# First mixers begin with two value units on unnormalised x, exact x made behind them; operands in PSUM, low parts cut to width

## What is computed

```python
def first_block(x, ...):                 # cut
    for l in range(2):
        x = x + 0.5 * swiglu(rmsnorm(x, ffn1_norm[l]), ffn1_w_in[l], ffn1_w_out[l])
        x = x + hybrid_mixer(rmsnorm(x, mix_norm[l]), w_in[l], ...)
        x = x + 0.5 * swiglu(rmsnorm(x, ffn2_norm[l]), ffn2_w_in[l], ffn2_w_out[l])

def second_block(x, mem, ...):           # cut
    for l in range(2):
        x = x + hybrid_mixer_2(rms_norm(x, mix_norm[l]), ...)
        x = x + memory_cross_attention(rms_norm(x, mem_x_norm[l]), mem, ...)
        x = x + conv_gated_ffn(rms_norm(x, ffn_norm[l]), ...)
    return rms_norm(x, final_norm)
```

## Time and profile before

| | |
|---|---|
| Median of 3 runs | 2544.12 us |
| Lowest, highest | 2541.17, 2551.29 us |
| The profiled execution | 2547.06 us |
| Its span on the core | 2545.1 us |
| Granted TensorE clock, mean | 0.98 |
| Busy over the span | PE 95%, PEld 89%, POOL 70%, ACT 44%, DVE 42% |

### The profile page before, as it was taken

How to read it: one execution, slowest core, us unless ns; L and a number is a source line. 1 busy time by engine, 2 the same in 40 slices (tenths; PEclk the granted TensorE clock), 3 DMA queues, 4 the chain that set the end, 5 groups by cost and what they waited for, 6 DMA issues and landing times.

```text
span 2545.1 us, 44193 instructions
## 1 busy us (share of the span) xinstructions
PE 2414.0 (95%) x17548; PEld 2261.2 (89%) x17548; DVE 1067.2 (42%) x1686; ACT 1117.8 (44%) x1255; POOL 1787.8 (70%) x1368
## 2 busy tenths in 40 slices
PE   7999999998999999999999899999899999899998
PEld 7998888997999899898889799998788999788997
DVE  4224555323422332345553242223425664423865
ACT  4334434446433433444443644345444335455333
POOL 6998444455799899864445678987446998545996
PEclk9999999999999999999999999999999999799999
DMA  6554322323455455442223345564224655323553
GB/s 232 178 184 151 111 94 92 105 94 116 149 188 191 161 191 188 153 141 95 90 93 108 125 133 166 181 202 121 89 95 133 198 181 159 100 71 112 180 191 115
DMA packets 312188, 359.88 MB, mean 141 GB/s; under 512 B 18636, under 2 KB 291072, under 8 KB 311936
## 3 DMA queue, kind: packets, MB, share of 16 engines
q1 hardware_dynamic: 311866, 358.01, 43.3%
q10 hardware_dynamic: 198, 0.06, 0.0%
HBM read 357.00 MB, written 1.05 MB: 141 GB/s over the span
## 4 chain that ended last, share of the span: by engine, by line
POOL 60%; issue 34%; PE 4%; ACT 1%; POOLq 1%; DVE 0%; DMA 0%; ACTq 0%; DVEq 0%
POOL sb_lo L483 60%; PE ps L516 4%; POOLq L490 0%; DMA sb_hcol<-in_dn_a_log 0%; POOLq L492 0%; ACT sb_hT_h L1139 0%; ACT L1125 0%; ACT L1124 0%; ACT sb_kT L1131 0%; ACT sb_hi L1366 0%; ACTq L354 0%; ACT sb_hi L1120 0%; DVE sb_qT L2134 0%; DVE sb_levels L2067 0%; DVE sb_levels L2072 0%
## 5 line engine op out<-in xcount | busy, mean ns | idle before, releaser
L483 POOL TENSOR_TENSOR sb_lo<-sb_raw,sb_hi 128x512 fp32r<-128x512 f32 x1364 | 1787.6, 1346 | 734.7 <-ACT sb_hi L1120 733.8
L516 PE MATMUL ps<-sb_hT_h,sb_hi 128*128 128x256 f32 x3268 | 946.3, 290 | 30.3 <-ACT sb_levels L1182 6.1
L1120 ACT ACTIVATE sb_hi<-sb_raw 128x2048 fp32r<-128x2048 f32 x341 | 652.2, 1914 | 728.4 <-PE ps L516 697.4
L516 PE MATMUL ps<-sb_hT_h,sb_lo 128*128 128x256 f32 x3268 | 927.5, 284 | 0.0
L516 PE MATMUL ps<-sb_hT_l,sb_hi 128*128 128x256 f32 x3268 | 927.4, 284 | 0.0
L516 PEld LDWEIGHTS ps<-sb_hT_h,sb_hi 128*128 128x128 f32 x3268 | 627.8, 192 | 46.6 <-issue 23.0
L516 PEld LDWEIGHTS ps<-sb_hT_h,sb_lo 128*128 128x128 f32 x3268 | 628.6, 192 | 3.6 <-issue 1.4
L516 PEld LDWEIGHTS ps<-sb_hT_l,sb_hi 128*128 128x128 f32 x3268 | 628.0, 192 | 0.0
L516 PE MATMUL ps<-sb_hi,sb_o_h 128*128 128x512 f32 (+1 forms) x848 | 305.6, 360 | 8.9 <-DVE sb_o_l L1671 3.0
L516 PE MATMUL ps<-sb_hi,sb_o_l 128*128 128x512 f32 (+1 forms) x848 | 302.1, 356 | 0.0
L516 PE MATMUL ps<-sb_lo,sb_o_h 128*128 128x512 f32 (+1 forms) x848 | 301.4, 355 | 0.0
(11 more groups left out here) (341 smaller groups left out, 3139.8 us busy)
## 6 DMA issues: line engine op xcount, KB each, us to landing
sb_raw<-in_ffn_w_in SPq DMA_DIRECT2D x88, 1024.0 KB, 5.1
sb_raw<-in_w_in SPq DMA_DIRECT2D x78, 1024.0 KB, 5.2
sb_raw<-in_ffn_w_out SPq DMA_DIRECT2D x44, 1024.0 KB, 4.9
sb_raw<-in_ffn_w_up SPq DMA_DIRECT2D x44, 1024.0 KB, 5.1
sb_raw<-in_ffn_w_down SPq DMA_DIRECT2D x22, 1024.0 KB, 4.9
sb_raw<-in_w_out SPq DMA_DIRECT2D x16, 1024.0 KB, 5.1
sb_raw<-in_w_branch_a SPq DMA_DIRECT2D x8, 1024.0 KB, 5.1
sb_raw<-in_w_branch_b SPq DMA_DIRECT2D x8, 1024.0 KB, 5.1
```

Of the source, the lines that this page charges most:

```text
L483: ins = nc.gpsimd.tensor_tensor(lo[:, slot, c], raw[:, slot, c], hi[:, slot, c].bitcast(F32), ALU.subtract)
L516: ins = mm(dst, s, m, start=first and n == 0, stop=last and n == 3 * len(pairs) - 1)
L1120: fn(hi[:, slot, :], raw[:, slot, :], ACT.Copy).then_inc(hi_ready, 1)
```

## The change

Line numbers of the new kernel are higher than the old ones.

**Entry.** The first FFN of a block also turns x inside its last down unit. ACT and DVE make high and low parts of gain times x in `o_h`, `o_l` (shifted by four blocks, `UNSCALED_AT`, since the last down unit reads the low ones). PE runs sv0 and sv1 on them, token by token; ACT applies the root when it takes them out, one scale per partition. Meanwhile x with gain and root is made in `exact` (an alias of `qT`) by DVE from the turned x still in PSUM and `row`, and ACT and DVE split it into `hT_h`, `hT_l` for the other units. `tok` scaled, the 16 later turns and the 20 warming transposes go away.

**Order.** `FIRST` is now sv0, sv1, q0, z0, b, k0, a, v0, q1: nine units, with q1 taken from the first round of `delta`. b's and a's chain stands between the convolutions of k0 and v0.

**PSUM.** `prod`, the silu of the second blocks, the roots of `pre_roots`, the merge, the output of `delta` and the decay row work in PSUM where they stood in SBUF.

**Widths.** `split` and the low parts run over the columns a unit has; POOL's loop over the ring is written out.

```diff
-FIRST = [("b", 0), ("a", 0), ("sv", 0)] + pair_units(0) + [("sv", 1)]
-DELTA_BG = [pair_units(1) + [("sv", 2), ("sv", 3)], pair_units(2) + [("sq", 0), ("sk", 0)],
+FIRST = [("sv", 0), ("sv", 1), ("q", 0), ("z", 0), ("b", 0), ("k", 0), ("a", 0), ("v", 0), ("q", 1)]
+DELTA_BG = [pair_units(1)[1:] + [("sv", 2), ("sv", 3)], pair_units(2) + [("sq", 0), ("sk", 0)],
...
+def mix1_width(r):
+    return KB * mix1_unit(r)[3] if r < MIX1_UNITS else UNIT
+MIX2_WIDTHS = [2048, 1280, 1536, 1536, 2048, 2048, 2048, 1152, 768] + [UNIT] * 12
...
-        sil, prod = xinv, yinv
+        sil, conv_sil, prod = xinv, ps[:, 2, :], ps[:, 3, :]
+        exact = qT
...
+            for u, width in enumerate(WIDTHS):
+                if u == 0:
+                    continue
+                slot = u % RING
+                pool.wait_ge(hi_ready, u + 1)
+                if u < RING:
+                    pool.wait_ge(lo_ready, RING + u)
+                pieces = -(-width // (UNIT // PIECES))
+                for i in range(pieces):
+                    c = slice(width * i // pieces, width * (i + 1) // pieces)
...
+            def unscaled_part(b, k, bank, q, k0, k1):
+                if k0 == 0:
+                    arrived(b, k)
+                w = weights(k, KB, 256)
+                for t in range(ST):
+                    tt_ = slice(t * P, (t + 1) * P)
+                    for c in range(k0, k1):
+                        if t == 0 and c % 2 == 0:
+                            pe.wait_ge(h_ready, 4 * q + (c // 2 + 1))
+                        for n, (o, wt) in enumerate(((o_h, w[0]), (o_l, w[0]), (o_h, w[1]))):
+                            ins = mm(ps[:, bank, t * S:(t + 1) * S], o[:, (c + UNSCALED_AT) % KB, tt_], wt[:, c, :],
...
             def mixer1(l, b, q):                                  # PE
+                unscaled_part(b, 0, 0, q, 0, 4)
+                pe.wait_ge(x_ready, updates(q))
+                for g in range(2, 4):
+                    turn(g, AFTER_FFN_BANKS[g])
+                unscaled_part(b, 1, 1, q, 0, 4)
+                turn_row(3 * l + 1, AFTER_FFN_ROW)
+                unscaled_part(b, 0, 0, q, 4, KB)
+                unscaled_part(b, 1, 1, q, 4, KB)
+                pe.wait_ge(bank_free[0], BANK_UNITS[0] * l + 1)
+                arrived(b, 2)
...
+                                pe.wait_ge(exact_low, 4 * l + (c // 2 + 1))
...
-                ffn(2 * l, b, sil_ready, 2 * NCH * l)
-                transposes(3 * l + 1, l)
+                ffn(2 * l, b, sil_ready, 2 * NCH * l, 3 * l + 1)
...
             def mixer1(l, b, gain):                               # ACT
+                take_row(q, AFTER_FFN_ROW)
+                for g in range(4):
+                    act.wait_ge(exact_ready, 4 * l + (g + 1))
+                    sl = slice(2 * g, 2 * g + 2)
+                    fn(hT_h[:, sl, :], exact[:, sl, :], ACT.Copy).then_inc(exact_high, 1)
+                    if g == 1:
+                        evac1(l, 0)
+                        mix_split(b, 3)
+                evac1(l, 1)
...
-                rsqrt(levels[:, 2:4, :], ps[:, 2:4, :], 1.0 if half < NPAIR else 1.0 / P).then_inc(pre_act, 1)
+                rsqrt(ps[:, 2:4, :], ps[:, 2:4, :], 1.0 if half < NPAIR else 1.0 / P).then_inc(pre_act, 1)
...
             def mixer1(l, b):                                     # DVE
+                exact_pair(0)
+                for g in range(4):
+                    if g < 3:
+                        exact_pair(g + 1)
+                    dve.wait_ge(exact_high, 4 * l + (g + 1))
+                    c = slice(2 * g, 2 * g + 2)
+                    tt(hT_l[:, c, :], exact[:, c, :], hT_h[:, c, :].bitcast(F32), ALU.subtract).then_inc(exact_low, 1)
...
                 elif kind == "wb":                                # DVE, evac1
-                    tt(k2(t1), vT[:, sl, :], src, ALU.mult).then_inc(bank_free[bank], 1)
-                    freed(l, r)
-                    own.link(tt(k2(t2), k2(t1), zT[:, sl, :], ALU.add))
-                    halve(o_h[:, sl, :], o_l[:, sl, :], k2(t2)).then_inc(merged_ready, 1)
+                    own.link(tt(src, vT[:, sl, :], src, ALU.mult))
+                    own.link(tt(src, src, zT[:, sl, :], ALU.add))
+                    halve(o_h[:, sl, :], o_l[:, sl, :], src).then_inc(merged_ready, 1)
+                    dve.wait_ge(merged_ready, NPAIR * l + (int(c) + 1))
+                    dve.sem_inc(bank_free[bank], 1)
```

More of the change, by code:

```diff
@@ L815, in delta @@
                 wa("osq")
-                mm(ps[:, 2, :], cc("ones"), sq[:, 0, :], start=True, stop=True).then_inc(dl_pe, 1)
+                for i in range(2):
+                    ins = mm(ps[:, 6 + i, S:2 * S], cc("ones"), sq[:, 0, i * S:(i + 1) * S], start=True, stop=True)
+                ins.then_inc(dl_pe, 1)
                 yield
@@ L870, in mixer1 @@
                 ins.then_inc(rows_pe, 1)
-                for r in range(4, len(FIRST)):
-                    unit1(l, b, r)
                 warm(2)
@@ L1138, in high_pair @@
                     k = 2 * g + i
-                    ins = fn(dst[:, k, :], ps[:, bank, i * S:(i + 1) * S], ACT.Copy, scale=gain(k))
+                    ins = fn(dst[:, (k + at) % KB, :], ps[:, bank, i * S:(i + 1) * S], ACT.Copy, scale=gain(k))
                 ins.then_inc(hh_ready, 1)
@@ L1205, in evac1 @@
                     dst = tok[:, :, S * c:S * (c + 1)]
+                    if c < 2:
+                        act.wait_ge(unit_done, RING * b_of(l) + (r + RING + 1))
+                        for t in range(ST):
+                            ins = fn(dst[:, t, :], v[:, t, :], ACT.Copy, scale=rstd[:, t:t + 1])
+                        ins.then_inc(bank_free[bank], 1)
+                        return
                 elif kind in arena:
@@ L1306, in stick, with with_units @@
                 yield
-            def with_units(steps, todo, b, evac):
+            def with_units(steps, todo, b, evac, split=split):
                 late = []
@@ L1330, in plain, with mixer1 @@
                     if r + 2 < MIX1_UNITS:
[L1331 removed]
+                        mix_split(b, r + 2)
                     evac1(l, r)
[L1334 to L1339 removed]
+            def mixer1(l, b, gain):
+                q = 3 * l + 1
+                mix_split(b, 0)
+                mix_split(b, 1)
+                for g in range(2):
+                    high_pair(q, g, gain, o_h, AFTER_FFN_BANKS[g], UNSCALED_AT)
+                squares(q)
+                for g in range(2, 4):
+                    high_pair(q, g, gain, o_h, AFTER_FFN_BANKS[g], UNSCALED_AT)
+                diagonal()
+                mix_split(b, 2)
+                take_row(q, AFTER_FFN_ROW)
[7 more added lines that the diff above has]
+                evac1(l, 1)
+                mix_split(b, 4)
+                mix_split(b, 5)
+                evac1(l, 3)
+                mix_split(b, 6)
+                act.wait_ge(unit_done, RING * b + (B_AT + RING + 1))
+                fn(beta_r[:, :], ps[0:HEADS, B_AT % 2, 0:S], ACT.Exp, scale=-1.0).then_inc(bank_free[B_AT % 2], 1)
+                mix_split(b, 7)
+                mix_split(b, 8)
+                act.wait_ge(rows_dve, ROWS_DVE.at(l, "y"))
                 y, e = sq[0:HEADS, 0, 0:S], sq[0:HEADS, 0, S:2 * S]
@@ L1348, in mixer1 @@
                 fn(d, d, ACT.Exp).then_inc(rows_act, 1)
-                plain(l, b, range(2, len(FIRST) - 1))
-                split(b, len(FIRST) + 1)
+                mix_split(b, len(FIRST) + 1)
                 pre_squares(l, 0)
@@ L1859, in mixer1, with exact_pair @@
                 y, e = sq[h8, 0, 0:S], sq[h8, 0, S:2 * S]
-                dve.wait_ge(start_loaded, 16)
-                dve.wait_ge(unit_done, RING * b + (1 + RING + 1))
-                ts(y, ps[h8, 1, 0:S], hcol[:, 0:1], None, ALU.add).then_inc(bank_free[1], 1)
-                freed(l, 0)
-                own.link(ts(beta_r[:, :], beta_r[:, :], 1.0, None, ALU.add))
+                gates = ps[h8, A_AT % 2, S:2 * S]
+                dve.wait_ge(row_ready, 3 * l + 2)
+                def exact_pair(g):
+                    for i in range(2):
+                        k = 2 * g + i
+                        ins = stt(out=exact[:, k, :], in0=ps[:, AFTER_FFN_BANKS[g], i * S:(i + 1) * S], scalar=vec1[:, V1_MIX + k:V1_MIX + k + 1],
+                                  in1=row[:], op0=ALU.mult, op1=ALU.mult)
+                    ins.then_inc(exact_ready, 1)
```

171 lines of the change are left out of this document (85 added, 86 removed).

## The result

The changed kernel takes **2528.15 us**, the median of 7 runs (2523.44 to 2529.36), against 2544.12 of the kernel before (7 runs). The ratio is 0.9931, with a 95% interval from 0.9918 to 0.9945: 0.7% faster. The times of the kernel before lie further apart (2541.12 to 2558.80) than those of the changed one. The profiled execution has a span of 2527.0 us at a mean granted clock of 0.985. PE is still busy 95% of it; POOL went from 70% to 67%, DVE from 42% to 38%.

The account below looks back on a forecast made before the run. PE, 95% busy, bounds the kernel through its work, its waits and the lower clock. Terms -3.1 - 3.5 - 1.5 - 5.2 - 1.3 - 1.4 = -16.0 on the profiled 2547.06 give 2531.1, so median 2528, range 2519 to 2538.

Parts of the forecast that it names:

- What bounds it: Whole kernel: PE, 95% busy, is the bound; time is its own work, its waits and the lower clock.
- its last sign of being wrong: Wrong if places where PE's waits shrink only hand them to the next matmul that waits for POOL; no size.
- the seven groups of the earlier trace: Groups in the table of PE's waits, 38 us together; the change was said to touch five.
- Part a: First FFN, `prod` in PSUM: cast and subtraction take about 0.69 each and PE's wait goes, -3.1 us.
- Part b: `stick`, roots in PSUM: PE's waits for `pre_norm` shorten by 1.75 us per layer, -3.5 in all.
- Part c: Merge in PSUM: PE's wait of 1.4 us for the last merge's cast and subtraction goes, -1.5.
- Part d: Second mixer, widths: shorter chain, -2.6 us per layer, -5.2 in all; PE's waits for POOL another -1.3.
- Part e: Entry to the first mixers: -2.1 us there, +1.4 in delta's first round, net -0.7 per mixer, -1.4 in all.
- The rival that was to end slower: Entry: a two-SBUF-operand subtraction for exact x is held beside POOL in each mixer; +27 gives 2555 us; chance 0.03.

Follow-up runs that it names:

- experiment 11: The kernel before, unchanged, run once more for a second trace: 2539.49 us, span 2537.6.
- experiment 3: Changed kernel with prod, silu, roots, merge and delta's output in SBUF again, entry and widths kept: 2540.93 us, ratio 0.9981.
- experiment 2: Changed kernel with all splits and low parts over the full 2048 columns again, POOL's loop still written out: 2555.96 us, ratio 1.0037.
- experiment 1: Changed kernel with the old entry, FIRST order and decay row put back, PSUM operands and widths kept: 2527.42 us, ratio 0.9928.
- experiment 8: Kernel of experiment 1 with DVE's loop over the second blocks' layers written out: 2526.18 us, ratio 0.9924.
- experiment 9: Changed kernel with q1 given back to delta's first round, eight units in FIRST: 2538.25 us in one run.
- experiment 10: Kernel of experiment 9 with 50 warming turns ahead of `pre` where it had 20: 2536.89 us in one run.
- experiment 5: Kernel of experiment 2 with one small-chain instruction, beta's 1 + e, written to PSUM from one SBUF operand: 2549.33 us, ratio 0.9997.

## Why the prediction was right, and where it was not

The predicted 2528 met the measured 2528.15. Its sum held because several terms were right and the errors cancelled; that it met to 0.2 us is luck, since the ratio is known to 0.13% either way, 3 us.

- **What bounds it** held: PE's waits, its clock and its own warming turns moved the time. But the shares were others. The prediction booked nearly all in waits; the groups that it priced did fall by 16.4, and 11.2 of that came back as other waits, which its last sign of being wrong had feared (of POOL, though most came back behind DVE). The clock, left to the range but for 0.1, is by my estimate the largest share (8.3). The change touches six of the seven groups of the earlier trace rows, not five.
- **Part a** (-3.1) is right in this trace (-3.4 up to the turn, no wait), but it is a value of the execution: experiment 11 has neither the 13.54 nor the wait. The right term would have been a chance times 3 us. The mechanism, the operand, is shown by 691 and 692 ns in all 44. Undisturbed casts did get slower, from 0.43 to 0.69, and nobody waited for them.
- **Part b** (-3.5): PE's waits fell by 3.7 (7.0 to 3.3), the stages by 5.5, clock included. Experiment 3 gives about 3 per layer. Right, at the low side.
- **Part c** (-1.5): the wait is gone, the stages are 2.0 shorter, and 12.4 in experiment 3. Right.
- **Part d** (-5.2, and -1.3 for POOL's waits): the chain from L2032's start to L2050's end took 13.2 where it took 15.9, so -2.7 for a predicted -2.6. The waits tell less, since L2050's stayed at 5.3: the clock rose (1.00 for 0.95 in layer 0, 0.95 for 0.87 in layer 1), and PE reached the wait sooner. The stages give -2.7 and -4.0, of which 2.7 in the last layer are the execution's (experiment 11): against that trace they are -2.7 and -1.3, so -4.0 for the predicted -5.2. By experiments 2 and 3 nearly all of it is due to the widths (7 us without them, 1.5 in layer 0 and none in layer 1 without PSUM). POOL's waits outside the entry fell by 1.8.
- **Part e** (-1.4): the entry came to 59.5 (predicted 60.4), with waits of 1.3 at q0 (2), 0.8 before v0 (0.7) and 1.7 before `pre` (3); the first round cost +1.5 (+1.4). The sum was right and a little dear, but the wait at q0 fits by luck. I had it in the middle of the unit, for exact x's last low part. PE waited at the unit's first matmul, 0.1 us after q0's low part was ready (220.15 + 1.72 = 221.87): two of POOL's four pieces took 1.7, where I had 1.28 for each. Exact x's last low part was ready at 224.1, 1.5 before PE needed it. And the 1.7 that I took for the clock of 0.87 is 1.5 by my own figures (13.0 - 11.5). What it left out made up for the rest: rounds two to four took 1 to 2 us longer per layer, and PE waited 2.2 at the second pass of the second blocks' loop. Experiments 1 and 8 put the whole entry at zero.

**Two steps failed without showing in the sum.** The first is the widths' value. I gave them -5.2 in the second mixer and nothing in the entry; taking them away costs 28 us. The new entry puts the small chain, with instructions of two SBUF operands, where POOL works without a pause for 32 pieces, 41.8 us, when every unit has 2048 columns. In the changed kernel b and a have half the columns, POOL pauses at 244.1, and the same instruction took 0.95. But it stands in a new unbroken run of POOL's all the same (15.8 us from 244.6 on), so a shorter run is not what let it through. The moment is a candidate: all 16 held instructions of the 14 traces began within 0.52 us of the start of one of POOL's pieces (0.12 in experiment 2), and of the 957 with all sources in SBUF that began later in a piece, as this one did (0.61), none lost more than 1.9 us. But 840 that began as early were not held either, so the moment alone does not decide, and no run varied it alone. The rival that was to end slower (chance 0.03) had the right mechanism and named the wrong instructions: L1948 took 1.21 on average and never more than 1.8 in any run. My arguments against it were of two kinds. That POOL runs dry while PE waits is true, and too late: it took 10 us. That L1671 never exceeds 1699 proved nothing about an instruction that meets POOL at another phase.

The second is q1. I booked it as work moved out of `delta`, at a price of 1.4 there. Experiments 9 and 10 show that it also covers the wait before `pre`: with it the wait is 1.7 and the clock stays at 1.00, without it 3.7 and 5.3 and the clock falls to its lower level, 4 us of each first round.

The rule of the Trainium skill ("SBUF — State Buffer", Who interferes with whom) that whoever issues first gets the shared pair for the whole instruction, and the other blocks, is stated for the 2-port modes, to which casts belong. I read it as one piece being the most that DVE loses. Holds of 7.4 to 13.5 us, each over only when POOL's run was, stand against that reading, for casts and for instructions with two SBUF inputs, of which that section says that they contend but not for how long. That an instruction with at most one SBUF input, outside those modes, does not contend agrees with the 12910 of experiment 5.

## What to carry to other kernels

Where VectorE's small instructions stand in a chain that TensorE waits for, look at what GpSimd runs beside them: two SBUF sources, or a cast within SBUF, can cost all that is left of GpSimd's unbroken run (up to 13.5 us here), and where it happens differs between executions of the same kernel. Take one source from PSUM, for every instruction of the chain and not only for the one that shows in the trace. Look at a run of GpSimd's from its start: a window that cuts it shows it too short. And take a second trace of the kernel before, before its waits become terms: two of them differed here by 7.5 us. And price a moved unit also by the wait that it covers: waits of 3.7 and 5.3 us ahead of a stretch of small matmuls cost 4 us more each through the clock.
